# Two fused transformer blocks in fp32: modulation gates spread from rows, half of the third modulation group summed along rows by VectorE

## What is computed

```python
mod_x = (silu(c) @ w_mod + b_mod)            # one row of 6 x 1024; the same for c_ctx
sh_m, sc_m, gt_m, sh_f, sc_f, gt_f = split(mod_x, 6)
hx = rms_norm(x, g_pre_mix) * (1 + sc_m) + sh_m          # and hc from ctx
qa, ka, va, qr, kr, vr, gr = split(hx @ w_in)
mix = merge_heads(attention(...), retention(...), gr) @ w_out
x_new = x + gt_m * rms_norm(mix, g_post_mix)
hf = rms_norm(x_new, g_pre_ffn) * (1 + sc_f) + sh_f
x_out = x_new + gt_f * rms_norm(swiglu(hf), g_post_ffn)
```

## Time and profile before

| | us |
|---|---|
| median of three runs | 1015.12 |
| the three runs | 1015.12, 1014.80, 1015.16 |
| the profiled execution, its own time | 1015.45 |
| its span, first to last instruction | 1013.7 |
| PE busy in the span | 995.3 (98%) |
| DVE busy | 584.6 (58%) |
| ACT busy | 495.8 (49%) |
| mean rate of the loads | 186 GB/s |
| mean granted TensorE clock | 0.998 |

### The profile page before, as it was taken

The page is one execution under the profiler, slowest core; times in us unless marked ns, Lnnn a source line. Parts: engine busy times, 40 slices in busy tenths (PEclk is TensorE's granted clock), DMA queues, the critical chain, the costliest instruction groups (busy, mean ns, idle before and its releaser), DMA issues.

```text
span 1013.7 us, 13246 instructions
## 1 busy us (share of the span) xinstructions
PE 995.3 (98%) x5164; PEld 810.6 (80%) x5164; DVE 584.6 (58%) x660; ACT 495.8 (49%) x603; POOL 0.2 (0%) x4
## 2 busy tenths in 40 slices
PE   7999999999999999999999999999999999999997
PEld 5777776778888888888888887888888878888885
DVE  5374768667555554565555665567774465555543
ACT  6473347656544443554444534663545554444432
POOL 0000000000000000000000000000000000000000
PEclk9999999999999999999999999999999999999999
DMA  9967653133655545475545465534244245555441
GB/s 373 419 272 297 274 218 126 43 121 128 213 203 173 199 169 205 166 259 174 199 166 193 166 222 182 195 125 147 102 166 166 81 147 192 198 177 202 166 166 42
DMA packets 26686, 188.32 MB, mean 186 GB/s; under 512 B 2960, under 2 KB 3216, under 8 KB 4112
## 3 DMA queue, kind: packets, MB, share of 16 engines
q1 hardware_dynamic: 26064, 185.24, 50.2%
q10 hardware_dynamic: 576, 2.43, 0.6%
HBM read 186.61 MB, written 1.05 MB: 185 GB/s over the span
## 4 chain that ended last, share of the span: by engine, by line
PE 93%; DMA 2%; DVE 2%; ACT 1%; issue 1%; SPq 1%; ACTq 0%; DVEq 0%
PE bank L1818 24%; PE bank L1820 24%; PE bank L1819 24%; DMA raw<-in_weights 2%; PE bank L2026 2%; PE bank L1862 2%; PE bank L1846 2%; PE bank L1924 2%; PE bank L1854 2%; PE bank L2292 1%; PE bank L1903 1%; PE bank L2390 1%; PE bank L2217 1%; PE bank L2168 1%; PE bank L2093 1%
## 5 line engine op out<-in xcount | busy, mean ns | idle before, releaser
L1156 DVE TENSOR_TENSOR w_lo<-raw,w_hi 128x2048 fp32r<-128x2048 f32 x148 | 338.6, 2291 | 267.6 <-ACT w_hi L641 267.4
L641 ACT ACTIVATE w_hi<-raw 128x2048 fp32r<-128x2048 f32 x148 | 283.7, 1918 | 268.1 <-PE bank L1820 217.4
L1818 PE MATMUL bank<-w_hi,hT_hi 128*128 128x512 f32 (+1 forms) x760 | 299.8, 394 | 0.0
L1820 PE MATMUL bank<-w_hi,hT_lo 128*128 128x512 f32 (+1 forms) x760 | 294.9, 388 | 0.0
L1819 PE MATMUL bank<-w_lo,hT_hi 128*128 128x512 f32 (+1 forms) x760 | 294.3, 387 | 0.0
L1818 PEld LDWEIGHTS bank<-w_hi,hT_hi 128*128 128x128 f32 x760 | 142.8, 188 | 33.0 <-issue 5.7
L1820 PEld LDWEIGHTS bank<-w_hi,hT_lo 128*128 128x128 f32 x760 | 142.7, 188 | 29.8
L1819 PEld LDWEIGHTS bank<-w_lo,hT_hi 128*128 128x128 f32 x760 | 143.0, 188 | 27.8 <-issue 0.2
L1818 PE MATMUL bank<-w_hi,gT_hi 128*128 128x512 f32 x264 | 103.4, 392 | 0.0
L1820 PE MATMUL bank<-w_hi,gT_lo 128*128 128x512 f32 x264 | 102.8, 389 | 0.0
L1819 PE MATMUL bank<-w_lo,gT_hi 128*128 128x512 f32 x264 | 102.7, 389 | 0.0
(11 more groups left out here) (310 smaller groups left out, 1008.1 us busy)
## 6 DMA issues: line engine op xcount, KB each, us to landing
raw<-in_weights SPq DMA_DIRECT2D x152, 1024.0 KB, 4.8
arena<-in_first_mods SPq DMA_DIRECT2D x8, 1024.0 KB, 14.9
memV<-in_own_mods SPq DMA_DIRECT2D x6, 1024.0 KB, 4.8
arena<-in_own_mods SPq DMA_DIRECT2D x6, 1024.0 KB, 6.9
arena<-in_const ACTq DMA_DIRECT2D x1, 1088.0 KB, 5.1
memV<-in_mem SPq DMA_DIRECT2D x1, 1024.0 KB, 6.4
x_res<-in_x SPq DMA_DIRECT2D x1, 1024.0 KB, 17.5
arena<-in_ctx SPq DMA_DIRECT2D x1, 1024.0 KB, 15.2
```

Of the source, the lines that this page charges most:

```text
L641: act.activation(w_hi[:, v_slot, :], raw[:, u_slot, :], ACT.Copy).then_inc(hi_ready, 1)
L1156: ins = dve.tensor_tensor(w_lo[:, v_slot, n], raw[:, u_slot, n], w_hi[:, v_slot, n].bitcast(F32), ALU.subtract)
L1818: pe.matmul(out, hi, rhi, start=start, stop=False)
L1820: return pe.matmul(out, lo, rhi, start=False, stop=stop)
```

## The change

1. The columns of `w_mod` are put in the order shift, scale, shift, scale, gate, gate. So group 2 is the two gates, `mod` keeps 32 columns, and `a_ffn` is computed behind `mod_columns(1)`.
2. Of group 2 PE does four units (16 to 19), the `VISITS` of `W_IN + 5` go, and of the 16 later units 12 are left. The other four rows-of-128 are summed by DVE in eight steps of 128 x 1024 (`mod_rows`), each a multiply-add with a column of `silu_c` as scalar. They stand between `low_to(W_IN + 6)` and `low_to(W_IN + 7)`. `mod_sums` on PE, ahead of unit 16, waits for all eight and adds the 128 partitions with four matmuls by ones.
3. GpSimd's queue loads the eight pieces (0.5 MB each) into four half buffers, the last four each after a step has freed the half buffer. After the eighth step it loads unit 16, and later units 18 and 19 (1 MB each).
4. `mod_T(2)`, `mod_columns(2)`, `gain_col` and the diagonals go. DVE reads `mod_row`, waits for `gate_rows` (bias and gains, 0.5 MB), adds and multiplies (128 x 512 each). SP issues that load right behind the one of unit `W_OUT + 1`. The two operations stand between `low_to(W_IN + 10)` and `low_to(W_IN + 11)`; `low_to(W_IN + 10)` itself moves behind the ropes of qa.
5. The four matmuls that spread the gates now have one contraction row each, at partitions 0, 32, 64 and 96. They stand behind `mix_out(1, 0)` instead of ahead of it. The order on ACT isn't changed.

```diff
-VISITS = {W_IN + 2: 2, W_IN + 3: 3, W_IN + 4: 3, W_IN + 5: 3, W_IN + 6: 3, W_IN + 7: 2}
+RING_SLOT = 2
+VISITS = {W_IN + 2: (0, 1), W_IN + 3: (0, 1, RING_SLOT), W_IN + 4: (0, 1, RING_SLOT), W_IN + 6: (1, RING_SLOT), W_IN + 7: (0, 1)}
+ROW_K = 4
+ROW_SLOTS = [0, 1, 2, 3, 1, 2, 3, 2]
...
+                if u == RAW_AT[("w", W_OUT + 1)]:
+                    sp.wait_ge(mod_used, MODS_ON_PE)
+                    sp.dma_start(gate_rows[:, 0, :], io["gate_rows"]).then_inc(sem("gates_loaded"), 16)
...
+        @block.gpsimd
+        def _(pool):
+            pool.wait_ge(mod_used, 2 * MOD_K)
+            for step in range(2 * ROW_K):
+                if row_before(step) >= 0:
+                    pool.wait_ge(sem("mod_step"), row_before(step) + 1)
+                pool.dma_start(row_mod[ROW_SLOTS[step]], io["row_mods"][step]).then_inc(sem(f"row_loaded{ROW_SLOTS[step]}"), 16)
+            pool.wait_ge(sem("mod_step"), 2 * ROW_K)
+            for n, (m, (at, slot)) in enumerate(OWN_MODS.items()):
+                if m >= 2 * MOD_K:
+                    pool.wait_ge(mod_used, mods_behind(at)[0])
+                    pool.dma_start(own_mods[slot], io["own_mods"][n]).then_inc(sem(f"last_mod_loaded{slot}"), 16)
...
+            def mod_rows():
+                for step in range(2 * ROW_K):
+                    slot, part, k = ROW_SLOTS[step], step // ROW_K, MOD_K - ROW_K + step % ROW_K
+                    total = row_mod[part]
+                    dve.wait_ge(sem(f"row_loaded{slot}"), 16 * row_loads(step))
+                    if step % ROW_K == 0:
+                        dve.tensor_scalar(total, row_mod[slot], silu_c[:, k, 0:1], None, ALU.mult).then_inc(sem("mod_step"), 1)
+                    else:
+                        dve.wait_ge(sem("mod_step"), step)
+                        dve.scalar_tensor_tensor(out=total, in0=row_mod[slot], scalar=silu_c[:, k, 0:1], in1=total,
+                                                 op0=ALU.mult, op1=ALU.add).then_inc(sem("mod_step"), 1)
             low_to(W_IN + 5)
-            low_to(W_IN + 7)
...
+            low_to(W_IN + 6)
+            mod_rows()
+            low_to(W_IN + 7)
...
-            low_to(W_IN + 10)
-            mod_columns(2)
-            dve.tensor_tensor(gain_col[:, 0, :], mod[:, 16:24, 0], col("g_post_mix"), ALU.mult)
...
+            low_to(W_IN + 10)
+            read_out(dve, ("mod_row", 2))
+            dve.wait_ge(sem("gates_loaded"), 16)
+            chain(dve.tensor_tensor(mod_row[:, :], mod_row[:, :], gate_rows[:, 0, 0:512], ALU.add))
+            dve.tensor_tensor(mod_row[:, :], mod_row[:, :], gate_rows[:, 0, 512:1024], ALU.mult).then_inc(sem("gates_ready"), 1)
             low_to(W_IN + 11)
...
-            for g in range(2):
-                gain_diagonal(g)
...
+            def mod_sums():
+
+                pe.wait_ge(sem("mod_step"), 2 * ROW_K)
+                b = free(pe, ("mod_row", 2))
+                for j in range(4):
+                    pe.matmul(b[32 * j:32 * j + 32, :], ones[:, 0:32], row_mod[j // 2][:, j % 2 * 512:j % 2 * 512 + 512],
+                              start=True, stop=False)
...
+                    if j == 4:
+                        mod_sums()
...
-                    if j == 6:
-                        mod_T(2)
...
-            for q in range(4):
-                if q % 2 == 0:
-                    pe.wait_ge(sem(f"gain_diag{q // 2}"), 1)
-                b = free(pe, ("gain_row", q))
-                pe.matmul(b[:, :], ones, gain_diag[q // 2][:, (q % 2) * 512:(q % 2 + 1) * 512], start=True, stop=True)\
-                    .then_inc(full_sem(("gain_row", q)), 1)
             for q in range(2):
                 read_out(pe, ("mixT", q))
             mix_out(1, 0)
+            pe.wait_ge(sem("gates_ready"), 1)
+            for q in range(4):
+                b = free(pe, ("gain_row", q))
+                pe.matmul(b[:, :], ones[32 * q:32 * q + 1, :], mod_row[32 * q:32 * q + 1, :], start=True, stop=True)\
+                    .then_inc(full_sem(("gain_row", q)), 1)
             mix_out(1, 1)
```

More of the change, by code:

```diff
@@ L88 @@
     STREAM.append(("w", _v))
-    for _n in range(VISITS.get(_v, 0)):
-        if _n == 2:
+    for _n in VISITS.get(_v, ()):
+        if _n == RING_SLOT:
             STREAM.append(("mod", _m))
@@ L120 @@
 _at = 0
[L121 removed]
+for _name, _n in [("g_pre_mix", 8), ("g_pre_ffn", 8), ("b_mod", 32),
                   ("ffn1_norm", 8), ("mix_norm", 8), ("xattn_norm", 8), ("mem_norm", 8), ("ffn2_norm", 8),
@@ L498, in two_blocks_kernel @@
         own_mods = [memV[:].rearrange("p b d -> p (b d)"), qrn_qan]
+        row_mod = [mod_sum[:, e * 1024:(e + 1) * 1024] for mod_sum in own_mods for e in range(2)]
+        row_before = lambda step: max([n for n in range(step) if ROW_SLOTS[n] == ROW_SLOTS[step]], default=-1)
+        row_loads = lambda step: sum(ROW_SLOTS[n] == ROW_SLOTS[step] for n in range(step + 1))
         hi_ready = sem("hi_ready")
@@ L971, in _ @@
             act.wait_ge(sem("ffn_cols"), 1)
-            split_T("ffn0T", shift=(a_ffn, mod[:, 24:32, 0]))
+            split_T("ffn0T", shift=(a_ffn, mod[:, 16:24, 0]))
             split_to(W_UP[0] + 3)
@@ L1364, in _ @@
             mod_columns(1)
+            chain(dve.tensor_scalar(a_ffn[:, :], mod[:, 24:32, 0], 1.0, None, ALU.add))
+            dve.tensor_tensor(a_ffn[:, :], a_ffn[:, :], col("g_pre_ffn"), ALU.mult).then_inc(sem("ffn_cols"), 1)
             for tile in (0, 1):
@@ L1615, in _ @@
             norm_scale(x, xn)
-            split_T("ffn0T", shift=(a_ffn, mod[:, 24:32, 0]), qs=[0, 1])
+            split_T("ffn0T", shift=(a_ffn, mod[:, 16:24, 0]), qs=[0, 1])
             low_to(W_UP[0] + 1)
-            split_T("ffn0T", shift=(a_ffn, mod[:, 24:32, 0]), qs=[2, 3])
+            split_T("ffn0T", shift=(a_ffn, mod[:, 16:24, 0]), qs=[2, 3])
             low_to(W_UP[0] + 3)
@@ L1914, in mod_unit @@
                     slot = OWN_MODS[m][1]
-                    loads = sum(s == slot and n <= m for n, (_, s) in OWN_MODS.items())
-                    pe.wait_ge(sem(f"own_mod_loaded{slot}"), 16 * loads)
+                    loads = sum(s == slot and n // MOD_K == 2 == m // MOD_K and n <= m for n, (_, s) in OWN_MODS.items())
+                    if loads:
+                        pe.wait_ge(sem(f"last_mod_loaded{slot}"), 16 * loads)
+                    else:
+                        pe.wait_ge(sem(f"own_mod_loaded{slot}"), 16 * sum(s == slot and n <= m for n, (_, s) in OWN_MODS.items()))
                     w = own_mods[slot]
@@ L2586, in lay_out @@
     w += swiglu(f("ffn2_gate_2")[0], f("ffn2_up_2")[0], f("ffn2_down_2")[0])
-    mods = [f("w_mod")[0][k * P:(k + 1) * P, g * UNIT:(g + 1) * UNIT] for g in range(N_MOD // MOD_K) for k in range(MOD_K)]
+    parts = (0, 1, 3, 4, 2, 5)
+    w_mod = np.concatenate([f("w_mod")[0][:, D * n:D * (n + 1)] for n in parts], axis=1)
+    b_mod = np.concatenate([f("b_mod")[0][D * n:D * (n + 1)] for n in parts])
+    gates = np.zeros((P, 1024), np.float32)
+    gates[0::32, 0:512] = b_mod[4 * D:].reshape(4, 512)
+    gates[0::32, 512:] = np.concatenate([f("g_post_mix").reshape(-1), f("g_post_ffn").reshape(-1)]).reshape(4, 512)
+    mods = [w_mod[k * P:(k + 1) * P, g * UNIT:(g + 1) * UNIT] for g in range(N_MOD // MOD_K) for k in range(MOD_K)]
     units = {"w": w, "mod": mods}
@@ L2607, in lay_out @@
         "first_mods": np.stack(mods[:MOD_K]), "own_mods": np.stack([mods[m] for m in OWN_MODS]),
+        "row_mods": np.stack([w_mod[k * P:(k + 1) * P, c:c + 1024] for c in (4 * D, 5 * D) for k in range(MOD_K - ROW_K, MOD_K)]),
+        "gate_rows": gates,
         "cols": np.concatenate([small[name] for name in COLS], axis=1),
```

36 lines of the change are left out of this document (16 added, 20 removed).

## The result

The changed kernel takes 1037.22 us (median of four runs, 1036.91 to 1039.46). The kernel before took 1014.96 in the same comparison: ratio 1.0224, 95% interval 1.0206 to 1.0242. It is 22 us slower, 7.5 us more than the 1029.7 forecast and 2.2 us outside the range. The profiled execution is the one of 1036.91 us, span 1034.9.

A forecast was written before the change was run, and what follows sets the result against it. PE, busy for 98% of the span, was taken as the bound. Terms of 1.1 + 5.5 + 5.5 + 2.5 = 14.6 us on a median of 1015.1 gave 1029.7 us, range 1020 to 1035.

The forecast's parts named there:

- the four legs: PE's stretches ending at the end of j = 6, fifth scores, `mix_out(1, 1)` and `ffn0T` transposes: +1.1, +5.5, +5.2, +2.5 us.
- part 2: Third modulation group: DVE's row steps and GpSimd's loads make unit 16 late, +1.1 us instead of a 2.7 us gain.
- E: The end of PE's visit j = 6, at 137.7 us before, from which the attention's delays are counted.
- Part 5: At `mix_out(1, 1)`: matmuls behind 6 us of PE idle time run slowly, +2.5 us (0 to 3.5).
- Part 1: Modulation visits on PE: less work, so PE reaches j = 4 2.7 us early if nothing holds it there.
- "Ends" of part 2: Limits for the row steps and loads: -2.7 us at SP's best, +5 with 1 us more on each of four loads.
- Part 3: Attention: DVE waits 6.15 us for the gates' load, first row maximum 7.1 us late, +5.5 us (4.5 to 7.5).
- Part 4: Mixer output: ACT splits `W_OUT + 3` only behind the gate copies, `mix_out(1, 1)` +5.2 us, with post-norm +5.5 (5 to 8.2).
- that rival: Behind `mix_out(1, 0)`: the gates' four one-row matmuls run one after the other, 1031 us at most; no chance of its own.
- The rival "full rate": At `mix_out(1, 1)`: PE restarts at full rate behind the idle time, 1027.2 us, chance 0.22.
- The slow GpSimd queue: Row pieces: four dependent loads each take 1 us more on GpSimd's queue, +4 us, 1034 us, chance 0.10.

## Why the prediction was wrong, point by point

**Direction and mechanisms: right.** The waits that it named stand in the trace: 6.25 us at `mix_out(1, 1)` ended by DVE's `w_lo` (forecast 6.2), 6.34 us of DVE at the gates (6.15), 2.98 at unit 16 (3.8, "2 to 5"). Three of the four legs came within 1.2 us.

**The step that failed is part 2's size: +1.1 us forecast, +7.4 measured at E.** Its chain of loads was nearly right. The last row step ended at 114.5 (forecast 114.0), and unit 16 landed 4.9 us behind its issue (5.8). Three things stood behind that, none of which was in the sum.
- *Units 18 and 19.* I gave them "9.5 us for 2 MB beside 1 MB of the ring" and at most 1 us of wait. The DMA view shows two ring tiles beside them, 2.10 MB, the first of which went ahead of both, and unit 19 took 12.7 us. PE waited 2.87. I had counted the ring's bytes too low and did not ask which bytes go first. The same bytes in SyncE's queue, with the units ahead of the ring, take the wait away: this is shown.
- *The rate behind 3 us of idle time.* Part 5 priced it for the 6 us gap only, and the sum took units 16, 17 and 19 at the rate of the earlier trace rows. They took 1.9 us each. Worth at least 2 us, shown by the filled gaps.
- *0.9 us for the copies of vr* (ACT, at 103.6) at PE's arrival, 2.7 us earlier than before; the visit that was taken out had covered them. Part 1 said "if nothing holds it there" and did not look. It is why `mod_T(1)` moved by 2.1 us and not 2.7. That reading is the trace's; no run isolates it.

"Ends" of part 2 were -2.7 and +5. Even the upper one was made of one error only, 1 us on each load. The 0.4 us of `mod_T(2)` that part 1 names is in no sum; with it the forecast would have been lower still.

**Part 3: +5.5 forecast, +6.7 measured.** The first row maximum came at 171.69, with E at 145.1: E + 26.6 against E + 26.4 forecast. What is over came behind it: PE waited 3.27 us, two groups ahead of the fifth scores, and ran three of the groups behind that slowly (1.75, 1.97 and 1.21 us where 1.13 and 1.09 are usual), about 1.6 us. Once more the price of a 3 us gap. The run with the early load gave back 6.4.

**Part 4: right.** +5.2 to the start of `mix_out(1, 1)`, measured 5.6. The four one-row matmuls took 1.14 us together, so they ran side by side, and that rival is out. `mix_out(1, 0)` started at the gained 2.0 us, ACT's four copies took 2.06.

**Part 5: +2.5 forecast, 1.9 measured** (1.6 by the run with the filled gap). About seven of the 24 matmuls start late, 0.43 us apart, and the rest at the full rate. The rival "full rate" is out. That the size came so near was partly luck: it was taken from the start of the program, where the matmuls are slow at a clock that reads 1.00, while here the clock's column does fall. The Trainium skill ("TensorE: Matmul & The Clock Gate", Part 1) has it that an idle TensorE falls to 1.2 GHz; this trace agrees (0.79 from 230 to 240 us). The prediction should have put that price as a possible one behind every gap that it forecast, and not behind the longest alone.

**The rivals.** The slow GpSimd queue (1034) was the nearest, but not by its mechanism: the four pieces whose loads wait for a step took 3.4, 3.9, 4.4 and 3.5 us, against 4 taken, and SyncE's queue needed 5.0, 5.0, 4.9 and 3.1 for the same four. What was slow were loads of the one queue that came behind, or beside, those of the other. The Trainium skill's figures for the queue ("DMA: Bandwidth & Descriptors", section on the anatomy of a DMA on the GpSimd path) gave an estimate of 3.2 us for a piece and 4.4 for a unit. Nearest to it were the loads with little beside them, 3.4 and 4.9 us; the first four pieces took 5.7 to 10.3 and the last two units 8.9 and 12.7, so as a forecast of this case the figures were too low.

## What to carry to other kernels

A second queue moved no more bytes here (4.2 MB in 14 us, as in one queue), and the tile that was needed next landed behind tiles that were needed later: put it into the same queue, ahead of them. Before an instruction is inserted into an engine's order, ask what the instruction behind it is and who waits for that: one line of ACT's order and one of SyncE's were 16 of the 22 us here. When a forecast holds several waits of about 3 us on TensorE, give the lower clock behind each of them a price and a chance. And where a wait is filled to test a cause, look whether the filling itself becomes the wait.

## What the runs showed of the hardware

**A gap of 3 us can cost TensorE its clock, but need not.** The same wait of 3.3 us at the same instruction, in the changed kernel and in the one with 44 zero-adding matmuls further on (timelines of PE, one fence each):

```profile
179.88 1.06 PE L2261 MATMUL bank<-fixed,arena 128*128 128x128 f32 x8 [3.27 <-ACT arena L743]
180.88 1.75 PE L2137 MATMUL bank<-arena 64*128 64x512 f32 x4
182.56 1.97 PE L2261 MATMUL bank<-fixed,arena 128*128 128x128 f32 x8
```

```profile
178.56 1.06 PE L2262 MATMUL bank<-fixed,arena 128*128 128x128 f32 x8 [3.28 <-ACT arena L743]
179.55 1.13 PE L2138 MATMUL bank<-arena 64*128 64x512 f32 x4
180.61 1.09 PE L2262 MATMUL bank<-fixed,arena 128*128 128x128 f32 x8
```

In the first the clock falls to the lower level (it reads 0.50, 1.2 GHz, from 182 to 184) more than 1 us behind the gap, and the work takes up to 1.8 times as long; in the second it stays at 2.4. In the run with 26 such matmuls even a wait of 3.76 us at unit 16 left the unit its 1.07 us, and the next one took 1.77. This goes with the scatter. The kernel before stays within 1.7 us over 25 runs. The kernel with 26 zero-adding matmuls, whose other gaps are open, spreads over 5.7 us, and its five times follow the mean granted clock: 1031.40 at 0.997, 1032.78 at 0.996, 1034.11 and 1034.42 at 0.994, 1037.12 at 0.991. With the third group's gaps filled, five runs lie within 1.3 us, though the 3.0 and 6.3 us gaps behind it are open.

**The clock also fell once behind a much shorter gap.** In the version with the gates in the gaps PE had done two groups of two one-row matmuls (1.13 us each) with 0.56 us of idle time between them when the rate fell. With the same groups and the same 0.56 us in the version without rows it did not fall. So it is one place in one profile, and no run isolates it.

**Four matmuls of one row in different row strips run side by side**: 1.14 us for four of 512 columns, where four of 128 rows took 3.76.
